# Sample queries broadcast by DMA from internal DRAM, and two moved pieces of issue order, in a two-layer decoder step on 8 cores

## The reference

```
for i in range(DEPTH):
    x = x + mixer(rmsnorm(x, g_mix[i]))
    x = x + mem_attend(rmsnorm(x, g_attn[i]), mem_k[i], mem_v[i], w_q[i], w_o[i])
    x = x + sq_relu_mlp(rmsnorm(x, g_ffn[i]), w_up[i], w_down[i])

def mem_attend(u, k, v, w_q, w_o):
    q = (u @ w_q) in 4 heads of 256
    p = softmax(q . k / 16 over the 256 memory rows)
    return (p . v) @ w_o
```

## Time and profile before

| | before |
|---|---|
| median of 3 runs | 1620.26 us (1619.46 to 1620.95) |
| the profiled execution | 1619.59 us |
| its slowest core, first to last instruction | core 5, 1618.0 us |
| its other cores | 1610.3 to 1616.3 us |
| mean granted PE clock, by core | 0.991 to 0.996 |
| PE busy | 1562.5 us, 97% |
| DVE busy | 864.4 us, 53% |
| ACT busy | 567.3 us, 35% |
| POOL busy | 113.8 us, 7% |
| DMA engines, mean of 16, of which queue 0 and queue 1 | 36.0% and 11.1% of the span |

### The profile page before, as it was taken

One profiled execution on the slowest core, in us unless ns is written; L12 is line 12 of the kernel. 1 busy time (PEld: TensorE's weight loads), 2 busy tenths in 40 slices (PEclk: granted clock), 3 DMA queues, 4 the chain that ended last, 5 costly groups with the idle time before them and its releaser, 6 DMA issues.

```text
span 1618.0 us, 28570 instructions; the slowest of 8 cores (1610.3 to 1618.0 us)
## 1 busy us (share of the span) xinstructions
PE 1562.5 (97%) x10218; PEld 901.6 (56%) x10218; DVE 864.4 (53%) x1924; ACT 567.3 (35%) x1071; POOL 113.8 (7%) x245
## 2 busy tenths in 40 slices
PE   4899999999999999999999998999999999999997
PEld 3775545555556655555555554555455655555565
DVE  5666775655443444445666665776565444442325
ACT  4756445541121221222133224543643112213453
POOL 2002121110000000000000001121010000000000
PEclk9899999999999999999999999999999999999999
DMA  8969793675537706066000009694555663000012
GB/s 225 208 113 165 163 177 71 127 144 83 85 65 131 123 1 105 10 96 110 1 1 1 1 1 168 116 202 103 120 118 73 98 105 53 14 1 1 40 65 107
DMA packets 87190, 145.15 MB, mean 90 GB/s; under 512 B 4350, under 2 KB 41470, under 8 KB 87036
## 3 DMA queue, kind: packets, MB, share of 16 engines
q0 software_dynamic: 67568, 84.08, 36.0%
q1 hardware_dynamic: 19484, 59.24, 11.1%
HBM read 212.42 MB, written 14.36 MB: 140 GB/s over the span
## 4 chain that ended last, share of the span: by engine, by line
PE 89%; DVE 4%; ACT 2%; issue 2%; DMA 2%; POOL 0%; DVEq 0%; ACTq 0%; SPq 0%; POOLq 0%
PE PS L292 85%; PE PS L296 3%; DVE MEM L327 3%; ACT MEM L319 2%; PE PS L301 1%; DMA MEM<-gv 1%; DMA MEM<-x 1%; DVE MEM L331 1%; ACT MEM L308 1%; DVE MEM L304 0%; DVE MEM L345 0%; POOL MEM L354 0%; DVEq L1409 0%; ACT MEM L343 0%; ACTq L1409 0%
## 5 line engine op out<-in xcount | busy, mean ns | idle before, releaser
L292 PE MATMUL PS<-MEM 128*128 128x416 bf16 (+7 forms) x8938 | 1477.5, 325 | 12.4 <-DVE MEM L331 5.3
L292 PEld LDWEIGHTS PS<-MEM 128*128 128x128 bf16 (+1 forms) x8938 | 828.7, 98 | 647.9 <-issue 54.8
L331 DVE TENSOR_TENSOR MEM<-PS,MEM 128x416 f32<-128x416 f32 (+6 forms) x558 | 312.2, 575 | 296.0 <-PE PS L292 260.7
L319 ACT ACTIVATE MEM<-PS 128x416 f32<-128x416 f32 (+5 forms) x469 | 238.7, 510 | 588.7 <-PE PS L292 578.6
L331 DVE TENSOR_TENSOR MEM<-MEM 128x416 bf16<-128x416 f32 (+3 forms) x282 | 160.4, 584 | 224.6 <-ACT MEM L319 205.3
L319 ACT ACTIVATE MEM<-MEM 128x416 bf16<-128x416 f32 (+9 forms) x299 | 184.9, 630 | 147.8 <-DVE MEM L331 112.8
L327 DVE SCALAR_TENSOR_TENSOR MEM<-MEM 128x416 bf16<-128x416 f32 (+7 forms) x322 | 177.0, 601 | 60.1 <-ACT MEM L319 50.2
L304 DVE SCALAR_TENSOR_TENSOR MEM<-MEM,PS 128x256 f32<-128x256 f32 x256 | 105.2, 420 | 60.1 <-PE PS L292 36.7
L296 PE MATMUL PS<-MEM 128*128 128x128 bf16 (+6 forms) x1096 | 75.2, 267 | 18.1 <-DVE MEM L339 7.3
L343 ACT COPY MEM<-PS 128x512 f32<-128x512 f32 (+3 forms) x73 | 39.1, 536 | 128.1 <-PE PS L292 111.8
L296 PEld LDWEIGHTS PS<-MEM 128*128 128x128 bf16 (+3 forms) x1096 | 52.9, 105 | 40.4 <-issue 39.3
(11 more groups left out here) (28 smaller groups left out, 137.7 us busy)
## 6 DMA issues: line engine op xcount, KB each, us to landing
MEM<-ck SPq DMA_DIRECT2D x64, 512.0 KB, 6.1
MEM<-cv POOLq DMA_DIRECT2D x64, 256.0 KB, 6.1
MEM<-w_down POOLq DMA_DIRECT2D x6, 2048.0 KB, 18.0
MEM<-x SPq DMA_DIRECT2D x16, 512.0 KB, 13.1
MEM<-w_kv POOLq DMA_DIRECT2D x4, 2048.0 KB, 18.4
MEM<-w_o POOLq DMA_DIRECT2D x4, 2048.0 KB, 25.0
MEM<-w_up POOLq DMA_DIRECT2D x32, 256.0 KB, 12.7
MEM<-w_up POOLq DMA_DIRECT2D x4, 2048.0 KB, 18.0
```

Of the source, the lines that this page charges most:

```text
L292: P.add(PE, "c", lambda e, o=out.ap, l=lhsT.ap, r=rhs.ap: e.matmul(out=o, lhsT=l, rhs=r, start=start, stop=stop), [lhsT, rhs], [out])
L319: P.add(ACT, "c", lambda e, o=out.ap, i=in_.ap: e.activation(out=o, in_=i, func=func, bias=bias, scale=sc), rd, [out])
L331: P.add(eng, "c", lambda e, o=out.ap, a=in0.ap, b=in1.ap: e.tensor_tensor(out=o, in0=a, in1=b, op=op), [in0, in1], [out])
```

## The change

The two matmuls per sample and their banks go. `QSAMP` writes QS to an internal DRAM tensor `qrows` by SP (`qst`), and a new `SDQ(b)` reads one row of it back with a stride-0 access over 128 partitions (2 KB each, 256 KB in all), also by SP, into one of two bf16 buffers; it waits for `qst` and for the buffer. SDQ(0) is issued right behind `qst`, SDQ(b+1) behind SDK(b+1), and the first of the MLP's samples behind `SDV(n_att)` at the end of O(4). `dot` now has both inputs in SBUF, in the order of the key buffers. `S` returns `den(3)` uncalled: it runs after QSAMP for tile 0, and after chunk 0 of the next O for the others. The rest of the norm in O goes from ec 6 to ec 7. In the convolution's last tile squares, column sums and rest go from chunks 2, 3, 5 to 1, 2, 3.

```diff
+    q_d = nc.dram_tensor("qrows", [2, NS, D], BF16, kind="Internal").ap()
...
-                if c == 2:
-                    if ti == NT - 1:
-                        norm_a(SEQS[1][0], BUF[0], parts=2)
-                    elif ti:
-                        conv_nA(ti + 1)
-                if c == (3 if ti else 0):
+                if c == 1 and ti == NT - 1:
+                    norm_a(SEQS[1][0], BUF[0], parts=2)
+                if c == 2 and 0 < ti < NT - 1:
+                    conv_nA(ti + 1)
+                if c == (0 if ti == 0 else 2 if ti == NT - 1 else 3):
...
-                if c == (5 if ti else 2):
+                if c == (2 if ti == 0 else 3 if ti == NT - 1 else 5):
...
+        QBU = [T(QS.off, BF16, [D]), T(U3OFF + 4 * 4096 + 2 * 4160 + 2 * TW * 4, BF16, [D])]
+        QBA = [QBU[0], T(VWO.off + 2 * 4160, BF16, [D])]
...
+            qst.append(dma(SP, DV(q_d[l]), QS(p=(0, NS)), "qst"))
+            SDQ(0)
...
-            den(3)
+            return lambda: den(3)
...
+        def SDQ(b):
+            dma(SP, (QBU if b < n_att else QBA)[b % 2](), DV(q_d[l, b:b + 1, :].broadcast_to([128, D])), f"qb{b % 2}", after=tuple(qst))
...
-            for h2 in range(2):
-                bk = nxt()
-                mm(PSv(bk, 0, 512), V(IDB.ap[0:NS, b:b + 1].broadcast_to([NS, 128]), IDB().ivs),
-                   QS(sl(h2 * 512, (h2 + 1) * 512), p=(0, NS)), True, True)
-                for x in range(2):
-                    for hh in range(2):
-                        h = 2 * h2 + hh
-                        kv = KS[(2 * b + x) % 4](sl(h * 256, (h + 1) * 256))
-                        dot(kv, kv, PSv(bk, hh * 256, (hh + 1) * 256), SS(b % 4, sl(x * 4 + h, x * 4 + h + 1)))
+            qb = (QBU if b < n_att else QBA)[b % 2]
+            for x in range(2):
+                for h in range(4):
+                    kv = KS[(2 * b + x) % 4](sl(h * 256, (h + 1) * 256))
+                    dot(kv, kv, qb(sl(h * 256, (h + 1) * 256)), SS(b % 4, sl(x * 4 + h, x * 4 + h + 1)))
...
                 SDV(b + 1)
+                SDQ(b + 1)
...
                 QSAMP()
+                den3()
...
-            S(k, mid_s)
+            den3 = S(k, mid_s)
...
-                def mid_k(ec, k=k):
+                def mid_k(ec, k=k, den3=den3):
+                    if ec == 0:
+                        den3()
...
-                        if ec == 6:
+                        if ec == 7:
                             N2b(k + 2) if k + 2 < NT else N3b(0)
...
         SDV(n_att)
+        SDQ(n_att)
```

More of the change, by code:

```diff
@@ L950, in attn_phase @@
         KSA = [T(WQK.off + i * 4096, F32, [D]) for i in range(4)]
+        qst = []
+        QBU = [T(QS.off, BF16, [D]), T(U3OFF + 4 * 4096 + 2 * 4160 + 2 * TW * 4, BF16, [D])]
+        assert QBU[1].off + QBU[1].nbytes <= RSTDE.off and su.top <= QBU[1].off
+        QBA = [QBU[0], T(VWO.off + 2 * 4160, BF16, [D])]
         VSA = [T(VWO.off + i * 4160, BF16, [2, 4, 258]) for i in range(2)]
```

## The result

The changed kernel took 1605.15 us (median of 4 runs, 1602.58 to 1606.49), the kernel before 1620.43 on the same chip: a ratio of 0.9905, 95% interval 0.9887 to 0.9922. That is 15.3 us faster; the forecast was 18. Lines of kernel.py are one higher than before: `mm` is L293, `mmx` L297, `dot` L305, `act` L320, `stt` L328, `tt` L332, `dma` L355. The profiled execution took 1606.49; its slowest core is core 2 with 1604.9, its fastest core 4 with 1589.7.

What follows compares the result with a forecast made beforehand. PE was taken as the bound, busy 97% of the span; 17.0 (spread pairs) + 2.4 (den(3)) + 0.5 (dot wait) + 0.5 (convolution) - 2.9 (norm waits) = 17.5 us off 1619.6 gave 1602; range 1596.5 to 1607.5.

Steps and rivals of the forecast that it cites:

- three signs of being wrong: DVE waits for `qrows`; a dot takes under 380 or over 480 ns; the attention gives back more than 5 us.
- The sum: Whole kernel: 17.0 + 2.4 + 0.5 + 0.5 - 2.9 = 17.5 us gained.
- the pairs' 9.0 in the MLPs: 17 of the 32 pairs of spread matmuls removed from PE lie in the two MLPs: 9.0 us that should stay gained.
- den(3)'s 2.4: End of S in the attention: PE's waits for ACT's Exp before den(3)'s matmuls go, 2.4 us gained.
- the six norm waits: PE's waits for DVE's norm in O: three at 1.2, three at 0.5, 5.1 us in all.
- The 2.2 of before: The same six norm waits before the change: about 2.2 us, 0.98 in three brackets, three hidden, and 0.16 each.
- I take no difference: DVE's dots with both inputs in SBUF last as long as with one in PSUM, 420 ns: no gain or loss.
- What den(3) now delays: Attention: den(3)'s later Ln, Exp and multiplications hold up DVE's additions, so PE's norm waits grow: 2.9 us lost.
- the rival *more: DVE keeps up and all six norm waits vanish instead of growing: 22.6 us gained, 1597 us; chance 0.18.
- Transfers get later and none late: cost 0: Query rows' added DMA traffic raises the engines' load from 0.80 to about 0.91 yet delays no reader: cost 0.
- Cover 9 us or more: Query rows have 21 us from issue to their dots, against transfers of 12.2 at most: 9 us or more spare.
- The convolution: Last tile's norm two chunks earlier: bank wait moves to chunk 6; gain 0.5 us, between 1 lost and 2.4 gained.

Runs made afterwards that it cites:

- dot_pace: The changed kernel with each dot again made to wait for the dot before it, by counting the query row as exclusively held: 1610.39 us, 0.9945 of before.
- row_place_late: The changed kernel with query-row places exchanged for layer 0's MLP samples and eight w_up pieces issued in the second and third MLP tile: 1596.45 us, 0.9861 of before.

## Why the prediction was nearly right

The time lay inside the range, 3 us above the forecast, but by two errors that cancelled in part; that it came so close is luck. Of its three signs of being wrong two came: DVE waited for `qrows`, and the attentions of core 2 gave back 10.5 us, more than 5. The third, a dot under 380 or over 480 ns, did not; but how long a dot takes was the wrong thing to watch.

**The sum held for the kernel that it assumed.** It said 17.5 us. dot_pace, where dots keep their old pace, gains 17.1 on a core that never waits for `cv`. Of that the pairs' 9.0 in the MLPs came as 4.9 and 4.4 (17 x 0.55), den(3)'s 2.4 as 2.7, and the six norm waits as forecast: the brackets of dot_pace sum to 4.2, with 0.16 each to 5.1, three of them near 1.2 and three near 0.5. (The 2.2 of before is loose: 0.98 and six times 0.16 are 1.9.)

**The step on the dots failed: "I take no difference".** The duration was right, 420 ns with either source. What counts is the distance from one dot to the next: 0.50 on the mean with the semaphore between two readers of a bank, 0.35 without, wherever the operand lies. I took 8 x 0.5 from the earlier trace rows and carried it over to a kernel whose dots have no bank to hold. With 0.35, DVE is 1.2 us further at every sample, and **the 2.9 us of "What den(3) now delays" did not come; the 2.2 of before went as well**: 5.0 us in dot_pace's difference, 5.1 by those terms. So an undisturbed core did what the rival *more* said, 22.1 of its 22.6 us, for another reason than any that the text gave. The earlier trace rows held the hint: 6.0 us of idle time ahead of a dot were put down to the dot before. The Trainium skill's 58 and 120 cycles for the two sources ("VectorE: DVE Perf Modes", section on the TRN2 errata), which by the prediction's estimate would make a dot 65 ns shorter, are not borne out: 420 ns with either. (The prediction's "my sum 3 us lower" there means a time 3 us lower, so a larger gain.)

**The step on the query rows failed: "Transfers get later and none late: cost 0".** The load was right, 0.93 for 0.91. But I followed only the rows and the keys to their readers. The values, in another queue, had 25 us and took 13 at most in this stretch before; with weight pieces ahead of them and the rows beside them they took 28. On core 2 that cost 10.5 us of the 22: 7.0 in three waits, and some 1.7 of low clock behind each of the two long ones. ("Cover 9 us or more" counted the keys' 12.2; by the 18.4 of the earlier trace rows it was under 3.) The rows themselves were in time but for two, 4.1 us of DVE's waits, both as layer 0's MLP begins. There a second thing was missed: a row that waits for its place stops SP's queue, and the keys behind it.

**The convolution**: 0.5 forecast; the waits moved as described, and the move is worth 0.2 to 0.3 on a core whose clock stays up, and a loss of 0.6 on the four others.

**Of the signs to watch for** these came: the 64 matmuls, ACT's waits gone, SA(2) later against its O(1), a bank wait in the convolution's last tile. These did not: brackets of 1 us in O(1) of both layers, and no wait of DVE for `qrows`.

## What to carry to other kernels

When an operand moves from one memory to another, look up what orders its readers, before and after, and count the distance between two of them in the timeline, not the duration of one. When a change adds transfers, list every transfer that shares the engines or the issuing queue, with its own time from issue to reader; the one with the longest cover can be the first to be late, since nobody watched it. A transfer whose target is still being read stops the queue behind it: give it a target that is free when it is issued.

## What the runs showed of the hardware

Two dots on DVE that a semaphore orders start further apart than two that none orders, though neither lasts longer: 0.53 to 0.61 us against 0.34 or 0.35, at 0.42 for each dot. The longer distance came with the operand in PSUM (before) and in SBUF (dot_pace), and so did the shorter one (before, the changed kernel).

A wait of PE may cost more than itself. On core 2 of the changed kernel the 3.93 us wait was followed by a granted clock of 0.60 (most of the stretch at the lower level, 1.2 GHz), the 2.81 us wait at 1098.91 by 0.59 (columns as in the earlier trace rows):

```profile
236.00:240.00 4.00, 0.53 (x8) 0.14 (x8) 3.01 (x17) 0.90 (x1) 0.00 (x0) 0.92 1.14 258
240.00:243.50 3.50, 3.50 (x17) 1.61 (x14) 0.44 (x1) 2.20 (x2) 0.00 (x0) 0.60 0.35 50
...
1098.90:1102.50 3.60, 3.59 (x19) 1.64 (x20) 1.13 (x5) 2.82 (x2) 0.00 (x0) 0.59 0.87 247
```

Core 6 had the same wait of 2.81 in the same place and no such stretch; the 64 matmuls behind it took 11.43 us there and 13.11 on core 2, 1.7 more. First core 2, then core 6:

```profile
1098.91 0.40 PE L297 MATMUL PS<-MEM 128*16 128x257 bf16 x8 [2.81 <-DMA MEM<-cv]
1099.24 13.11 PE L293 MATMUL PS<-MEM 128*128 128x416 bf16 x64
```

```profile
1090.23 0.40 PE L297 MATMUL PS<-MEM 128*16 128x257 bf16 x8 [2.81 <-DMA MEM<-cv]
1090.57 11.43 PE L293 MATMUL PS<-MEM 128*128 128x416 bf16 x64
```

The convolution's bank wait, 1.98 or 1.99 us, was followed by such a stretch on four of eight cores in the changed kernel (0.56 to 0.65 in the 3.6 us behind it), on seven in row_place_late, and on none before, where it was longer, 2.25. What decides it, no run here settles.
